# Two-layer hybrid decoder on one core: unnormalised rows into TensorE, inverse root mean squares applied as products leave PSUM, output projection and routing block by block

## The reference

```python
def rms_norm(x, g):
    y = xf * lax.rsqrt(jnp.mean(xf * xf, axis=-1, keepdims=True) + EPS)
    return (y * g).astype(x.dtype)
for layer in range(2):
    h = rms_norm(x, g_mix[layer])
    proj = h @ w_in[layer]                 # 1024 -> 5936, split in ten parts
    # attention (norms of c_q, c_kv and of the heads), gated linear attention, pooling
    merged = sum(sigmoid(gate_logits) * (branches @ w_branch[layer]))
    x = x + merged @ w_out[layer]
    h = rms_norm(x, g_ffn[layer])
    x = x + swiglu(h, ...)                 # layer 0, dense, width 2816
    x = x + moe_ffn(h, ...)                # layer 1, top 2 of 8 experts, width 1408
# swiglu: (silu(h @ w_gate) * (h @ w_up)) @ w_down
# moe_ffn: logits = h @ w_router, top 2, softmax of the two, weighted sum of the experts
```

## Time and profile before

| | |
|---|---|
| median of 3 runs | 1156.89 us (1156.83 to 1158.81) |
| the profiled execution | 1159.74 us, its span 1158.0 us |
| TensorE busy | 1091.9 us, 94% of the span |
| VectorE busy | 826.0 us, 71% |
| ScalarE busy | 672.9 us, 58% |
| GpSimd busy | 74.0 us, 6% |
| mean granted TensorE clock | 0.977 of full speed |

### The profile page before, as it was taken

The page is one execution under the profiler, slowest core; times in us unless marked ns, Lnnn a source line. Parts: engine busy times, 40 slices in busy tenths (PEclk is TensorE's granted clock), DMA queues, the critical chain, the costliest instruction groups (busy, mean ns, idle before and its releaser), DMA issues.

```text
span 1158.0 us, 16888 instructions
## 1 busy us (share of the span) xinstructions
PE 1091.9 (94%) x6535; PEld 942.8 (81%) x6535; DVE 826.0 (71%) x1116; ACT 672.9 (58%) x964; POOL 74.0 (6%) x119
## 2 busy tenths in 40 slices
PE   4999999998999999899999996899999999999996
PEld 3978787777999998888787775887888888888885
DVE  3577856875544545457966786489898989989895
ACT  3467745454434434466754544477677676777763
POOL 4000521000000000000622000000000000000000
PEclk9999999998999999999999997699999999999999
DMA  5554354555546535254344446389899999999992
GB/s 175 194 174 144 110 166 129 179 196 204 166 163 223 195 128 188 67 181 146 119 148 144 162 156 227 109 299 364 275 355 346 323 331 324 379 323 366 337 344 85
DMA packets 147670, 250.19 MB, mean 216 GB/s; under 512 B 5166, under 2 KB 108676, under 8 KB 147588
## 3 DMA queue, kind: packets, MB, share of 16 engines
q1 hardware_dynamic: 145808, 246.89, 62.9%
q10 hardware_dynamic: 1780, 2.19, 0.6%
HBM read 248.02 MB, written 1.05 MB: 215 GB/s over the span
## 4 chain that ended last, share of the span: by engine, by line
PE 81%; DVE 12%; ACT 4%; issue 2%; POOL 1%; DMA 1%; ACTq 0%; DVEq 0%; POOLq 0%
PE PS L619 26%; PE PS L1073 9%; PE PS L1074 9%; PE PS L1075 9%; PE PS L935 5%; PE PS L936 5%; PE PS L937 5%; DVE w_lo L399 4%; PE PS L707 2%; DVE m_lo L1755 2%; PE PS L1033 1%; PE PS L645 1%; ACT w_hi L390 1%; PE PS L802 1%; PE PS L1045 1%
## 5 line engine op out<-in xcount | busy, mean ns | idle before, releaser
L399 DVE TENSOR_TENSOR w_lo<-ring,w_hi 128x1536 fp32r<-128x1536 f32 (+1 forms) x192 | 310.3, 1633 | 116.8 <-ACT w_hi L390 116.6
L390 ACT ACTIVATE w_hi<-ring 128x1536 fp32r<-128x1536 f32 (+1 forms) x192 | 264.7, 1387 | 143.7 <-PE PS L937 86.0
L1755 DVE TENSOR_TENSOR m_lo<-ring,m_hi 128x512 fp32r<-128x512 f32 (+2 forms) x256 | 185.9, 755 | 91.6 <-ACT m_hi L1270 90.0
L1270 ACT ACTIVATE m_hi<-ring 128x512 fp32r<-128x512 f32 (+2 forms) x256 | 157.5, 631 | 141.3 <-PE PS L619 138.9
L619 PE MATMUL PS<-m_hi,h_hi 128*128 128x512 f32 (+2 forms) x352 | 125.8, 357 | 2.1 <-DVE m_lo L1755 2.1
L1073 PE MATMUL PS<-w_hi,hTe 128*96 128x384 f32 (+1 forms) x384 | 126.5, 329 | 0.7 <-issue 0.7
L1074 PE MATMUL PS<-w_hi,hTe 128*96 128x384 f32 (+1 forms) x384 | 124.9, 325 | 0.0
L1075 PE MATMUL PS<-w_lo,hTe 128*96 128x384 f32 (+1 forms) x384 | 124.8, 325 | 0.0
L619 PE MATMUL PS<-m_lo,h_hi 128*128 128x512 f32 (+2 forms) x352 | 121.0, 344 | 0.0
L619 PE MATMUL PS<-m_hi,h_lo 128*128 128x512 f32 (+2 forms) x352 | 121.0, 344 | 0.0
L935 PE MATMUL PS<-h_hi,w_hi 128*128 128x256 f32 x352 | 100.7, 286 | 0.8 <-DVE h_lo L1737 0.8
(11 more groups left out here) (321 smaller groups left out, 2199.3 us busy)
## 6 DMA issues: line engine op xcount, KB each, us to landing
ring<-in_w_in_dram SPq DMA_DIRECT2D x40, 1024.0 KB, 5.2
ring<-in_w_exp_gate_dram SPq DMA_DIRECT2D x24, 1536.0 KB, 7.6
ring<-in_w_exp_up_dram SPq DMA_DIRECT2D x24, 1536.0 KB, 9.2
ring<-in_w_exp_down_dram SPq DMA_DIRECT2D x24, 1536.0 KB, 7.9
ring<-in_w_branch_dram SPq DMA_DIRECT2D x12, 1024.0 KB, 5.0
ring<-in_w_ffn_gate_dram SPq DMA_DIRECT2D x6, 1536.0 KB, 6.7
ring<-in_w_ffn_up_dram SPq DMA_DIRECT2D x6, 1536.0 KB, 7.3
ring<-in_w_ffn_down_dram SPq DMA_DIRECT2D x6, 1536.0 KB, 6.3
```

The lines of the kernel that those rows point to most:

```text
L390: act.activation(split_parts(u, j)[0], ring[:, i % NSLOT, w0:w0 + words], ACT.Copy)\
L399: dve.tensor_tensor(lo, ring[:, (j // 2) % NSLOT, w0:w0 + words], hi.bitcast(F32), SUB).then_inc(sem(f"lo_ready{b}"), 1)
L1270: act.activation(hi, raw, ACT.Copy).then_inc(sem("m_hi_ready"), 1)
L1755: dve.tensor_tensor(lo, raw, hi.bitcast(F32), SUB).then_inc(sem("m_lo_ready"), 1)
```

## The change

1. **Norms 0, 1 and 2** lose their place ahead of the products. VectorE multiplies rows by the gain alone (`gained`), which are transposed and split at once. The squares and the root (`squared`, `roots`) and the inverse come later. The inverses are laid out along the free dimension by one product with a diagonal matrix (`spread`, `rnb`), and are multiplied in as products leave PSUM: in `glr`, `gq`, `gk`, `gvt`, in the pooling input (now on VectorE, `pool_in`), as the scale of ScalarE's activations for the latents, gates and output gates, in `rg`, and in dense by a new VectorE step for each tile ahead of Silu (`gate_scaled`). The dense down product is scaled by row as it is added to x.
2. **Norm 3**: the rows that are transposed for the logits are `x_tok` itself, the gain is multiplied into the router weights once, the gathered rows are `gained`, and 16 products of one column (`row_scales`) put the inverses in the order of each expert's tokens; Silu takes them as its scale.
3. **Output projection** in the order out0, out2, out1, out3. `turn_merged(1)` is issued inside out0. Column half 0 of x is transposed inside out1, half 1 after out3, inside it (layer 1), or inside the first product of dense.
4. **Dense to mixer 1**: block 0 is transposed ahead of the last half of the down product, block 1 inside `va`.
5. **Routing** goes by token blocks: logits, the two largest, ranks and selection of block 0 while TensorE makes those of block 1. The selection is first built for the first two experts alone; halves 1 and 2 of the first expert's weights are subtracted after the gather, the other selections after that.
6. **Start**: x is loaded in two halves, the second behind the first weights, and the gain is the first transfer of ScalarE's queue.

```diff
@@ -122,7 +123,7 @@
 
 LOADS = (["va", "vb", "cq", "ckv", "gq", "gk", "uq", "oga", "ukv", "ogb", "ua", "ub"]
          + [f"g{i}" for i in range(5)] + ["pool"] + [f"g{i}" for i in range(5, 12)]
-         + ["br00", "br01", "br20", "br21", "br10", "br11"] + ["out0", "out1", "out2", "out3"])
+         + ["br00", "br01", "br20", "br21", "br10", "br11"] + ["out0", "out2", "out1", "out3"])
 NL = len(LOADS)
...
 
                 w = 2 * L + (which == "hf")
-                for c in range(2):
-                    bank, full = begin(L, f"{which}{a}{c}")
-                    pe.wait_ge(sem("xn_ready"), 4 * w + 2 * a + c + 1)
-                    for i in range(4):
-                        mm = pe.transpose(bank[:, i * P:(i + 1) * P], xn[:, a, (4 * c + i) * P:(4 * c + i + 1) * P], ident[:, :])
-                    mm.then_inc(full, 1)
+                bank, full = begin(L, f"{which}{a}{c}")
+                if w == 2 * DEPTH - 1:
+                    evacuated(L, f"w{c}{a}")
+                    rows = x_tok
+                else:
+                    pe.wait_ge(sem("xn_ready"), norm_block(w, a, c) + 1)
+                    rows = xn
+                for i in range(4):
+                    mm = pe.transpose(bank[:, i * P:(i + 1) * P], rows[:, a, (4 * c + i) * P:(4 * c + i + 1) * P], ident[:, :])
+                mm.then_inc(full, 1)
+
+            def spread(w):
+
+                if w == 1:
+                    pe.wait_ge(sem("gate_free0"), gate_no(1, 0))
+                pe.wait_ge(sem("diag_ready"), w + 1)
+                pe.matmul(PS[:, 6, 0:T], ones[:, :], rdiag, start=True, stop=True).then_inc(sem("rnb_full"), 1)
 
...
                 bank, full = begin(L, "va")
                 token_after_token(L, "va", [bank[:, a * 256:(a + 1) * 256] for a in range(TT)], [None, full],
-                                  first=lambda a: turn_h(L, "hm", 1) if a else None)
+                                  between={(0, 2): [(L, "hm", 1, 0)], (1, 0): [(L, "hm", 1, 1)]}, source="hm")
                 if L == 0:
                     parameters()
                 vb = by_tokens(L, "vb")
...
                 w0 = [begin(L, f"w0{a}") for a in range(TT)]
                 evacuated(L, "mt00"), evacuated(L, "mt01")
-                out_part(0, w0)
-                turn_merged(1)
-                w1 = [begin(L, f"w1{a}") for a in range(TT)]
-                out_part(1, w1)
+                out_part(0, w0, lambda: turn_merged(1))
                 evacuated(L, "mt10"), evacuated(L, "mt11")
                 out_part(2, w0)
+                w1 = [begin(L, f"w1{a}") for a in range(TT)]
+                out_part(1, w1, turn_first_half)
                 out_part(3, w1)
-                for a in range(TT):
-                    turn_h(L, "hf", a)
+                if L < DEPTH - 1:
+                    turn_h(L, "hf", 0, 1)
 
             def mixer_left(L, b):
...
+                        spread(1)
                 if not first:
                     for a in range(TT):
                         for j in range(HALVES - NSPLIT, HALVES):
+                            if a == 1 and j == HALVES - 1:
+                                turn_h(1, "hm", 0, 0), turn_h(1, "hm", 0, 1)
                             mm = down(a, j, *parts(dense_unit(u), j))
                             if a == 1:
...
-            pe.wait_ge(sem("router_in"), 16)
+            for a in range(TT):
+                pe.wait_ge(sem(f"gate_free{a}"), gate_no(2, 0))
+            pe.wait_ge(sem("router_ready"), 1)
+
+            def logits(a, c):
+
+                evacuated(1, f"hf{a}{c}")
...
+            logits(1, 1).then_inc(sem("logits_full"), 1)
+
             for b in range(NB):
                 mixer_left(1, b)
-            for a in range(TT):
-                pe.wait_ge(sem(f"gate_free{a}"), gate_no(2, 0))
-            for i in range(KD):
-                for a in range(TT):
-                    mm = pe.matmul(PS[:, 0, a * NE:(a + 1) * NE], hT[:, i, a * P:(a + 1) * P], wr[:, i, :],
-                                   start=(i == 0 and a == 0), stop=(i == KD - 1), skip_group_check=True)
-            mm.then_inc(sem("logits_full"), 1)
-
+            first_rank, second_rank, totals = (PS[:, b, 0:NE] for b in RANK_BANKS)
+            pe.wait_ge(sem("tri_ready"), 1)
             pe.wait_ge(sem("msel_ready"), 1)
-            pe.wait_ge(sem("tri_ready"), 1)
-            pe.matmul(PS[:, 1, 0:NE], tri[:, :], msel[:, 0, :], start=True, stop=True)
-            pe.matmul(PS[:, 1, NE:2 * NE], ones[:, :], msel[:, 0, :], start=True, stop=False)
-            pe.matmul(PS[:, 1, NE:2 * NE], tri[:, :], msel[:, 1, :], start=False, stop=True)
-            pe.matmul(PS[:, 1, 2 * NE:3 * NE], ones[:, :], msel[:, 0, :], start=True, stop=False)
-            pe.matmul(PS[:, 1, 2 * NE:3 * NE], ones[:, :], msel[:, 1, :], start=False, stop=True)\
-              .then_inc(sem("rank_full"), 1)
+            pe.matmul(first_rank, tri, msel[:, 0, :], start=True, stop=True).then_inc(sem("rank_full"), 1)
+            pe.matmul(second_rank, ones[:, :], msel[:, 0, :], start=True, stop=False)
+            pe.matmul(totals, ones[:, :], msel[:, 0, :], start=True, stop=False)
+            pe.wait_ge(sem("msel_ready"), 2)
...
+            def row_scales(r):
+
+                pe.wait_ge(sem("psel_ready"), 4 * r + 4)
+                pe.wait_ge(sem("rn_set"), 2 * DEPTH)
+                for e in range(NE):
+                    for a in range(TT):
+                        mm = pe.matmul(PS[0:CAP, 6, e:e + 1], psel[:, a, e, :].bitcast(F32), inv_rms(2 * DEPTH - 1, a),
+                                       start=(e == 0 and a == 0), stop=(a == TT - 1), skip_group_check=True)
+                mm.then_inc(sem("rsl_full"), 1)
+
             def prepare(r, part):
...
-                load_gain(2 * L + 1)
-                split(L, "out1", LAST)
-                split(L, "out2")
-                split(L, "out3")
-
+                split(L, "out2", LAST)
+                split(L, "out1")
+                split(L, "out3", FIRST)
+                high(w + 1, 0, 0), high(w + 1, 1, 0)
+                split(L, "out3", LAST)
+                if L == DEPTH - 1:
+                    token_high(0, 0), token_high(1, 0)
                 for j in range(2):
                     round_hi(act, (L, 0), j, L, 0)
-                load_sqrt()
-                norm(2 * L + 1)
...
+
+                    x = x_tok[:, a, c * 512:(c + 1) * 512]
+                    dve.scalar_tensor_tensor(x, PS[:, 4 + 2 * a + c, :], inv_rms(w - 1, a), x, MUL, ADD).then_inc(sem("x_dense"), 1)
+                    dve.wait_ge(sem("x_dense"), 2 * a + c + 1)
+
+                if L:
+                    dve.wait_ge(sem("down_full"), 1)
+                    x_dense(0, 0), x_dense(0, 1)
+                gained(w, 0, 0), gained(w, 0, 1)
+                low(w, 0, 0), low(w, 0, 1)
+                if L:
+                    wait_used(dve, dense_unit(NDENSE - 1), HALVES - 1)
+                    x_dense(1, 0), gained(w, 1, 0), x_dense(1, 1), gained(w, 1, 1)
+                else:
+                    split(L, "va")
+                    gained(w, 1, 0), gained(w, 1, 1)
+                low(w, 1, 0), low(w, 1, 1)
                 split(L, "vb")
+                inverse(w), diagonal(w)
                 v_half("va", 0)
                 split(L, "cq", FIRST)
...
 
+                def pool_in(i, name):
+
+                    bank, free = full(L, name)
+                    dve.tensor_tensor(u[:, 2 * i:2 * i + 2, PADW:PADW + T], two(bank), every(rnb[:, :], 2), MUL).then_inc(free, 1)
+
...
                 merge(1, 2), merge(1, 3)
                 split(L, "out0", LAST)
+                split(L, "out2", FIRST)
+                merged_low(2), merged_low(3)
+                split(L, "out2", LAST)
                 split(L, "out1", FIRST)
-                merged_low(2), merged_low(3)
+                x_plus(0, 0)
                 split(L, "out1", LAST)
-                split(L, "out2")
-                split(L, "out3")
-
-                def x_plus(c, a):
-                    bank, free = full(L, f"w{c}{a}")
-                    x = x_tok[:, a, c * 512:(c + 1) * 512]
-                    dve.scalar_tensor_tensor(x, bank, 0.5, x, MUL, ADD).then_inc(free, 1)
-                x_plus(0, 0), x_plus(0, 1)
-                for j in range(2):
-                    rest_lo(dve, (L, 0), j)
-                norm(2 * L + 1, lambda a: x_plus(1, a))
-                rest_lo(dve, (L, 0), 2)
+                x_plus(0, 1)
+                gained(w + 1, 0, 0), gained(w + 1, 1, 0)
+                split(L, "out3", FIRST)
+                if L < DEPTH - 1:
+                    low(w + 1, 0, 0), low(w + 1, 1, 0)
+                    split(L, "out3", LAST)
+                else:
+                    split(L, "out3", LAST)
+                    token_low(0, 0), token_low(1, 0)
+                rest_lo(dve, (L, 0), 0)
+                x_plus(1, 0), gained(w + 1, 0, 1)
+                x_plus(1, 1), gained(w + 1, 1, 1)
```

(57 more changed lines are left out.)

355 lines of the change are left out of this document (209 added, 146 removed).

## The result

| | before | after |
|---|---|---|
| median | 1157.85 us (1156.83 to 1159.66, 4 runs) | 1128.65 us (1128.09 to 1131.52, 4 runs) |
| the profiled execution | 1159.74 us, span 1158.0 | 1128.09 us, span 1126.1 |
| TensorE busy, idle | 1091.9, 66.1 us | 1083.9, 42.2 us |
| VectorE, ScalarE busy | 826.0, 672.9 us | 837.6, 680.7 us |
| mean granted clock | 0.977 | 0.989 |

The ratio is 0.9746, its 95% interval 0.9732 to 0.976. The prediction, 1126 (1118 to 1134), was right, and its sum, made against the profiled execution, said 1128.8 where 1128.09 came. TensorE lost 23.9 us of idle time, and 8.0 us of busy time too, though it makes 38 instructions more.

The account below looks back on a forecast made before the run. It took TensorE, busy 94% of the span, as the bound. 7.2 + 9.4 + 6.4 + 9.9 - 1.3 - 0.4 - 0.3 = 30.9 us off the profiled execution gave 1128.8, scaled to the median 1126 (1118 to 1134, 8 in 10).

Parts of the forecast that it names:

- Bound: Whole kernel: TensorE, busy 94% of the span, is the bound; only its idle time, added work and clock move the end.
- Start: Norm 0: gain and half of x loaded first, products from 10.9, va ending at 19.5; gain 7.2 us (5.5 to 8).
- Norm 1: Mixer 0 to dense: norm work hidden under the reordered quarters, 0.7 stall at out2; gain 9.4 us (8 to 10).
- Gate scaling in dense: Dense: gate_scaled adds 8.4 us on VectorE, covered by TensorE's standing four tiles, so it costs nothing.
- Norm 2: Dense to mixer 1: va ends at 467.5 instead of 473.93, TensorE waiting 0.3 for block 1; gain 6.4 us (5 to 6.7).
- Out3 reached 1.6 later: Mixer 1, ahead of routing: 0.7 stall and 0.9 of transposes moved ahead make out3 start 1.6 us later.
- Routing: Out3 to gather: 1.6 stall, gather 14.2 us after out3's start, at 713.8 against 728.00; gain 14.1 us.
- The experts: First expert to the end: row_scales costs 3.5 us, clock and small hand-overs 1.5; -5.0 in all.
- Rival A: Routing: the clock stays up, giving the gather 2.4, the first expert 2.8, the rest 1.5; 1119 us; chance 16%.
- Rival B: Routing: the clock falls early, slowing logits and row_scales by 3.5 each, one more stretch by 1; 1134 us; chance 18%.
- Rival C: Experts: slot 0's later refill makes the weight stream the bound, 1159 us with the low bounds; chance 3%.
- Rival D: All norms: their waits are replaced by equally long waits for x_plus and splits, no effect, 1157 us; chance 1%.

Follow-up runs that it names:

- e4: The changed kernel with VectorE starting block 0's two largest only when both blocks' logits are complete; 1129.18 us, 0.9746 of the kernel before.
- e3: The changed kernel with 14 more VectorE multiplications of a PSUM tile in dense, result unused; 1126.9 us, 0.9732 of the kernel before.
- e7: The changed kernel with three pieces of vb rounded ahead of the parameters' copy in layer 0; 1127.33 us, 0.9727 of the kernel before.
- e12: The changed kernel with three orders changed and ten products of 384 zero columns put into the routing; 1119.12 us, 0.9658 of the kernel before.
- e1: The changed kernel with norm 0's gain loaded behind the nine small parameter loads again; 1135.98 us, 0.9793 of the kernel before.
- e5: The kernel before with norm 0's gain loaded first on ScalarE's queue, x still in one load; 1157.64 us, 0.9991 of the kernel before.

## Why the prediction was right, and where its terms were off

- **Bound.** Right. TensorE's idle time and clock moved the end, and every edit of the changed kernel that moved one of TensorE's waits moved the end of the span, if not always by as much (e4: 1.14 at the gather, 0.8 at the end). The 14 scalings that e3 adds on VectorE moved nothing.
- **Start**, 7.2 predicted, 6.29 came: first product 11.34 for 10.9, `va`'s end 20.47 for 19.5. The mechanism, `va`'s arrival as the bound, is the row at 9.93, 0.4 later than assumed. What the prediction left out is the 2.08 us between `va` and `vb`, which it left standing as it was; e7 shows that it was an order and no transfer. It stood before the change too, so it is a gain not seen and no error of the sum.
- **Norm 1**: 8.95 for 9.0, the stall ahead of out2 0.45 for 0.7. **Gate scaling in dense** 0 for 0. The 0.87 in dense are 0.79 for block 0's transposes of norm 2, which now stand in the down product. The prediction counted them nowhere.
- **Norm 2** is thus 6.54 - 0.79 = 5.75 for 6.4, with one wait of 0.58 for the 0.3.
- **Out3 reached 1.6 later**: right. In mixer 1 TensorE waits 0.6 us more for `Pr`, in mixer 0 no more than before; the prediction did not see it, and why it comes in the one and not in the other stays open.
- **Routing**: 15.15 for 15.8; the stall in out3 1.62 for 1.6, the gather 14.8 after out3 for 14.2, because the last eight logit products took 2.3 and not 1.8, as the clock fell in them.
- **The experts**, -1.74 for -5.0, is the term that was mis-sized, in four parts: `row_scales` 2.66 for 3.5 (83 ns a record; the bound of 2.6 for 96 columns was the right one); +1.7 where -1.2 was allowed for the clock, since of the first expert 2.6 us ran at 1.2 GHz (702.61 to 705.2) and not 6.0; -0.35 at the end, where the clock falls 7.9 us before the last instruction and the last four products take 0.63 to 0.77 instead of 0.40 to 0.50 (TensorE ends 0.7 later, 0.35 of which reaches the end of the span); and -0.4 between these, which no mark here places.
- **Rival A** (the clock stays up) did not come. The low stretch shrank from 34.1 to 13.6 us, but it still covers the whole gather; of what A would give beyond the forecast, only 1.7 of the 2.8 of the first expert came. The Trainium skill's page "TensorE: Matmul & The Clock Gate", section "Why this matters for your kernels", asks for no long idle gap between bursts. This case doesn't agree that this is enough: in e12 it fell within continuous work. **Rival B** did not come: 27 of the 32 logit records started at 2.4 GHz, and all of `row_scales` ran at it. **Rival C** has the right date and no effect: slot 0 was refilled at 705.10, 2.5 us after the first expert's first product, as worked out (2.4), and by the second expert the stream was as far as before (an issue 46.8 us into the experts for 45.7). No rounding of weights waits for a transfer in that stretch, in a trace with 0.93 of the DMA engines' time taken. So 0.92 and 0.93 of that time did not mean here that TensorE would wait for weights. **Rival D** is excluded by every mark of the table.
- **The sum** is right partly because errors cancel: start, dense, mixer 1 and routing came out 2.6 us worse than forecast, the experts 3.3 better. The last step, 0.9975 from the profiled execution to the median, took the number from 1128.8 to 1126, away from the 1128.65 that came: the profiled execution after does not lie above its median.

## What to carry to other kernels

When a value that is needed late (here an inverse root mean square) stands in a chain that TensorE waits for, taking it out pays only with the loads and the order of the products arranged so that nothing else ends at the same point: the late norm was worth 0.9 us at the start with the gain loaded late (e1 against before) and 6.0 with the gain and half of x first (e5 against the changed kernel, x in one load in e5), and of the 22.5 us won around norms 1 and 3, 12.3 went when the quarters were put back in their old order, with all of the algebra in place. Count what a moved step issues at its new place, and look at the list of the engine that serves (VectorE, ScalarE) for work put ahead of what TensorE waits for; three such orders gave 10 us more. For waits of 2 us and more, look in several executions whether the clock fell behind them, and add it to the price.
